# A layer norm's first two weight pieces, token tile by token tile, with splits, squares and roots in other places

## The reference

```
u = rmsnorm(x, norm_mix);  proj = u @ w_in          # then attention, convolution, gates
x = x + merged @ w_mix_out
u = rmsnorm(x, norm_mlp)
x = x + square(relu(u @ w_mlp_up)) @ w_mlp_down
```

## Time and profile before

| | us |
|---|---|
| median of 3 runs | 1827.13 (1826.56 to 1827.42) |
| the profiled execution, its own time | 1827.84 |
| its span | 1826.4 |
| PE busy in the span | 1733.0 (95%) |
| mean granted TensorE clock, as a share of 2.4 GHz | 0.978 |

### The profile page before, as it was taken

One profiled execution on the slowest core, in us unless ns is written; L12 is line 12 of the kernel. 1 busy time (PEld: TensorE's weight loads), 2 busy tenths in 40 slices (PEclk: granted clock), 3 DMA queues, 4 the chain that ended last, 5 costly groups with the idle time before them and its releaser, 6 DMA issues.

```text
span 1826.4 us, 33244 instructions
## 1 busy us (share of the span) xinstructions
PE 1733.0 (95%) x11638; PEld 1592.1 (87%) x11638; DVE 1352.7 (74%) x2358; ACT 911.6 (50%) x1601; POOL 63.8 (3%) x116
## 2 busy tenths in 40 slices
PE   6999899998999899988988999999999999999996
PEld 5999799988899788977867999999999978888885
DVE  5985778876876678868665699997888856666665
ACT  3344344443354434443544455567777644455543
POOL 0000011000000112100000000000000000000000
PEclk9999999998999999998988999999999999999999
DMA  5655587753544599852325355554344455555553
GB/s 200 206 191 181 177 301 270 264 189 117 168 150 161 179 337 299 268 185 82 116 81 184 128 177 179 184 185 150 130 137 138 136 167 193 195 192 189 194 194 138
DMA packets 92041, 333.87 MB, mean 183 GB/s; under 512 B 11048, under 2 KB 11224, under 8 KB 91504
## 3 DMA queue, kind: packets, MB, share of 16 engines
q1 hardware_dynamic: 80064, 289.06, 47.1%
q0 software_dynamic: 10912, 39.38, 6.5%
q10 hardware_dynamic: 976, 4.19, 0.6%
HBM read 330.46 MB, written 6.07 MB: 184 GB/s over the span
## 4 chain that ended last, share of the span: by engine, by line
PE 78%; DVE 14%; ACT 3%; issue 3%; DMA 2%; DVEq 0%; SPq 0%; ACTq 0%
PE bank L199 23%; PE bank L200 23%; PE bank L201 23%; DVE Z L84 6%; DVE w_lo L180 4%; PE bank L1617 3%; DMA raw<-stream 1%; PE bank L249 1%; ACT w_hi L178 1%; ACT space L84 1%; PE bank L1226 1%; DVE st L84 1%; DVE x L84 1%; DVE u_lo L84 1%; PE bank L453 1%
## 5 line engine op out<-in xcount | busy, mean ns | idle before, releaser
L180 DVE TENSOR_TENSOR w_lo<-raw,w_hi 128x1024 fp32r<-128x1024 f32 x546 | 661.4, 1221 | 183.2 <-ACT w_hi L178 181.6
L178 ACT ACTIVATE w_hi<-raw 128x1024 fp32r<-128x1024 f32 x546 | 573.9, 1052 | 289.0 <-PE bank L201 212.1
L199 PE MATMUL bank<-u_hi,w_hi 128*128 128x256 f32 x2416 | 703.6, 291 | 9.4 <-DVE w_lo L180 3.5
L201 PE MATMUL bank<-u_hi,w_lo 128*128 128x256 f32 x2416 | 688.7, 285 | 0.0
L200 PE MATMUL bank<-u_lo,w_hi 128*128 128x256 f32 x2416 | 688.7, 285 | 0.0
L199 PEld LDWEIGHTS bank<-u_hi,w_hi 128*128 128x128 f32 x2416 | 469.2, 194 | 23.8 <-issue 10.6
L200 PEld LDWEIGHTS bank<-u_lo,w_hi 128*128 128x128 f32 x2416 | 468.6, 194 | 4.7 <-issue 2.4
L201 PEld LDWEIGHTS bank<-u_hi,w_lo 128*128 128x128 f32 x2416 | 468.2, 194 | 0.0
L199 PE MATMUL bank<-w_hi,a_hi 128*128 128x512 f32 x768 | 300.7, 391 | 3.7 <-DVE a_lo L936 1.8
L200 PE MATMUL bank<-w_lo,a_hi 128*128 128x512 f32 x768 | 300.2, 391 | 0.0
L201 PE MATMUL bank<-w_hi,a_lo 128*128 128x512 f32 x768 | 299.5, 390 | 0.0
(11 more groups left out here) (263 smaller groups left out, 1659.4 us busy)
## 6 DMA issues: line engine op xcount, KB each, us to landing
raw<-stream SPq DMA_DIRECT2D x546, 512.0 KB, 3.3
gate<-w_ada POOLq DMA_DIRECT2D x48, 512.0 KB, 6.5
space<-b_ada POOLq DMA_DIRECT2D x6, 512.0 KB, 4.6
t_rows<-t_by_distance POOLq DMA_DIRECT2D x8, 256.0 KB, 3.9
rpb_rows<-rpb_pad POOLq DMA_DIRECT2D x8, 224.0 KB, 3.9
gains<-gains POOLq DMA_DIRECT2D x3, 512.0 KB, 4.8
bias_a<-t_rows POOLq DMA_DIRECT2D x1, 1536.0 KB, 11.1
bias_b<-rpb_rows POOLq DMA_DIRECT2D x16, 96.0 KB, 7.9
```

The source lines that it names most:

```text
L178: nc.scalar.activation(w_hi[:, s, :], raw[:, s, :], ACT.Copy).then_inc(s_hi, 1)
L180: nc.vector.tensor_tensor(w_lo[:, s, :], raw[:, s, :], w_hi[:, s, :].bitcast(F32), ALU.subtract).then_inc(s_split, 1)
L199: M.matmul(o, lh, rh, start=start, stop=False, skip_group_check=True)
L201: return M.matmul(o, ll, rh, start=False, stop=stop, skip_group_check=True)
```

## The change

- `first_pieces` and `token_tile_b` take the place of `piece_b` for the two pieces behind each of the four layer norms: piece 1 over tile 0, piece 2 over tile 0, piece 1 over tile 1, piece 2 over tile 1. Each matmul has 128 moving columns, so there are 96 in place of 48.
- `second_tile`, a generator that is advanced behind each of the two tile 0 parts, issues the rest: first the split of a held piece's successor, the transposes and squares of tile 1 or 0; then the second transposes, the other splits and squares. `split` of the held pieces' slots is thereby issued later.
- `squares` comes ahead of the two pieces' end; `token_roots` stays behind them.
- The transposes of tile 0 come one held piece earlier where three are held.
- At the start x is loaded in two DMAs of 512 KB by token tile, not in four of 256 KB.
- The two `held_pieces` calls of the second block issue their splits after the held pieces instead of among them; only PE instructions lie between the two places.

```
+        def token_tile_b(o, s, tt, ready):
+
+            cols = slice(tt * P, (tt + 1) * P)
+            for k in range(KD):
+                PE.wait(*ready[tt][k // 4])
+                i = mm3(o[:, cols], w_hi[:, s, k * P:(k + 1) * P], w_lo[:, s, k * P:(k + 1) * P],
+                        u_hi[:, k, cols], u_lo[:, k, cols], k == 0, k == KD - 1)
+            return i
+
+        def first_pieces(outs, ready, beside):
+
+            c, marks = at["piece"], []
+            for j, o in enumerate(outs):
+                nc.tensor.wait_ge(s_split, dyn(RING) + (c + j + 1))
+                token_tile_b(o, (c + j) % RING, 0, ready)
+                next(beside)
+            for j, o in enumerate(outs):
+                i = token_tile_b(o, (c + j) % RING, 1, ready)
+                at["piece"] += 1
+                marks.append(used(i))
+                if j:
+                    split(c + j + AHEAD)
+            return marks
...
                         i.then_inc(s_used, 1)
-                        if j < count - 1:
-                            split(c + AHEAD + 1 + j)
-                        if j == count - 2:
-                            late()
+                        if j == count - 1:
+                            bank_marks[NT - 1][1] = (s_used, dyn(RING) + (c + count))
+                        next(steps, None)
                 if tt == 0:
-                    halfway()
-            bank_marks[NT - 1][1] = (s_used, dyn(RING) + (c + count))
+                    next(steps, None)
+            return c + AHEAD + 1, count - 1
...
-            held_pieces(count, lhs, acc, lambda: (tile(0, 0), tile(0, 1)),
-                        lambda: turn_chunk(0, 0, gained[0, 0], ready))
-            turn_chunk(0, 1, gained[0, 1], ready)
+            def steps():
+                tile(0, 0), tile(0, 1)
+                yield
+                turn_chunk(0, 0, gained[0, 0], ready)
+                lower_next()
+                yield
+                if count > 2:
+                    turn_chunk(0, 1, gained[0, 1], ready)
+                    yield
+
+            beside = steps()
+            c, waiting = held_pieces(count, lhs, acc, beside)
+            if count == 2:
+                turn_chunk(0, 1, gained[0, 1], ready)
             lower_next()
             tile(1, 0)
+            tile(1, 1)
+            return ready, second_tile(ready, gained, marks, list(range(c, c + waiting + 1)))
+
+        def second_tile(ready, gained, marks, splits):
+
+            if splits:
+                split(splits.pop(0))
             turn_chunk(1, 0, gained[1, 0], ready)
+            squares(x, space_junk, 5, marks, 0)
             lower_next()
-            tile(1, 1)
-            lower_next()
+            yield
             turn_chunk(1, 1, gained[1, 1], ready)
             lower_next()
-            return ready, marks
+            while splits:
+                split(splits.pop(0))
+            got_sums[0] = squares(x, space_junk, 5, marks, 1)
+            yield
...
-        load_x(0, 0)
+        nc.sync.dma_start(x[:, 0, :], x_in[0:P, :]).then_inc(s_x[0], 16)
         nc.sync.dma_start(gains[:, 0, :], gains1[0:1, :].partition_broadcast(P).rearrange(
             "p a n -> p (a n)")).then_inc(s_gain0, 16)
         nc.sync.dma_start(kept[:, :], kept_in).then_inc(s_kept, 16)
-        load_x(1, 0)
         load_first(0)
-        load_x(0, 1)
-        load_x(1, 1)
+        nc.sync.dma_start(x[:, 1, :], x_in[P:2 * P, :]).then_inc(s_x[1], 16)
         for s in range(1, RING):
...
-        u_ready = [() for _ in range(KD)]
+        x_marks = [[(s_x[tt], 16)] * 2 for tt in range(NT)]
+        u_ready, gained = [[(), ()], [(), ()]], {}
+        space_junk = work[:, :, :].rearrange("p a n -> p (a n)")
         for n in range(2):
-            for tt in range(NT):
-                m = gain_chunk(x, gains[:, 0, :], tt, n, (s_gain0, 16), x_marks[tt][n])
-                turn_chunk(tt, n, m, u_ready)
-                if n or tt:
-                    lower_next()
-            if n == 0:
-                split(0)
+            m = gain_chunk(x, gains[:, 0, :], 0, n, (s_gain0, 16), x_marks[0][n])
+            turn_chunk(0, n, m, u_ready)
+            if n:
+                lower_next()
         lower_next()
-        for c in range(1, AHEAD):
-            split(c)
+        split(0)
+        for n in range(2):
+            gained[1, n] = gain_chunk(x, gains[:, 0, :], 1, n, x_marks[1][n])
+        first_u = u_ready, second_tile(u_ready, gained, x_marks, list(range(1, AHEAD + 1)))
...
-                take(4)
-                m = piece_b([bank[4][:, 0:T]], *U, ready=u_ready)
+                take(4), take(5)
+                m, iq_m = first_pieces([bank[4][:, 0:T], bank[5][:, 0:T]], *first_u)
...
-                for tt in range(NT):
-                    m = squares(x, work[:, :, :].rearrange("p a n -> p (a n)"), 5, x_marks, tt)
-                yield
-                m = token_roots(m)
+                m = token_roots(got_sums[0])
...
-            up(0, tile0 + 0, True)
-            up(1, tile0 + 1, True)
-            for tt in range(NT):
-                m = squares(x, work[:, :, :].rearrange("p a n -> p (a n)"), 5, x_marks, tt)
+            for q, m in enumerate(first_pieces([bank[4][:, 0:T], bank[5][:, 0:T]], *first_u)):
+                up(q, tile0 + q, m)
+            m = got_sums[0]
```

More of the change, by code:

```diff
@@ L235, in run @@
                 pass
-        ss_marks, norm_late, junk_mark = [], [], [None]
+        ss_marks, norm_late, junk_mark, got_sums = [], [], [None], [None]
         free = {}
@@ L315, in turn_chunk @@
                        bank[b][:, :].rearrange("p (k n) -> p k n", k=4), ACT.Copy)
-            norm_late.append((b, n, rows, m1, i, ready))
+            norm_late.append((b, n, tt, m1, i, ready))
         def lower_next():
-            b, n, rows, m1, i, ready = norm_late.pop(0)
+            b, n, tt, m1, i, ready = norm_late.pop(0)
+            rows = slice(tt * P, (tt + 1) * P)
             m = VE.go((m1, i), V.tensor_tensor, u_lo[:, 4 * n:4 * n + 4, rows],
@@ L323, in lower_next, with held_pieces @@
             free[b] = (m1, m)
-            for k in range(4 * n, 4 * n + 4):
-                ready[k] += (m1, m)
-        def held_pieces(count, lhs, acc, halfway, late):
+            ready[tt][n] = (m1, m)
+        def held_pieces(count, lhs, acc, steps):
             c, slots = at["piece"], []
@@ L347, in held_pieces @@
                         i.then_inc(s_used, 1)
-                        if j < count - 1:
-                            split(c + AHEAD + 1 + j)
-                        if j == count - 2:
-                            late()
+                        if j == count - 1:
+                            bank_marks[NT - 1][1] = (s_used, dyn(RING) + (c + count))
+                        next(steps, None)
                 if tt == 0:
-                    halfway()
-            bank_marks[NT - 1][1] = (s_used, dyn(RING) + (c + count))
+                    next(steps, None)
+            return c + AHEAD + 1, count - 1
         def added_and_gained(count, lhs, acc, x, gain, scale=None):
-            ready, marks, gained = [() for _ in range(KD)], [[None, None], [None, None]], {}
+            ready, marks, gained = [[(), ()], [(), ()]], [[None, None], [None, None]], {}
             def tile(tt, n):
@@ L606, in build @@
         store_ada(ADA_PER_LAYER - 1)
-        x_marks = [[(s_x[2 * tt + n], 16) for n in range(2)] for tt in range(NT)]
-        u_ready = [() for _ in range(KD)]
+        x_marks = [[(s_x[tt], 16)] * 2 for tt in range(NT)]
+        u_ready, gained = [[(), ()], [(), ()]], {}
+        space_junk = work[:, :, :].rearrange("p a n -> p (a n)")
         for n in range(2):
-            for tt in range(NT):
-                m = gain_chunk(x, gains[:, 0, :], tt, n, (s_gain0, 16), x_marks[tt][n])
-                turn_chunk(tt, n, m, u_ready)
-                if n or tt:
-                    lower_next()
-            if n == 0:
-                split(0)
+            m = gain_chunk(x, gains[:, 0, :], 0, n, (s_gain0, 16), x_marks[0][n])
+            turn_chunk(0, n, m, u_ready)
+            if n:
+                lower_next()
         lower_next()
-        for c in range(1, AHEAD):
-            split(c)
+        split(0)
+        for n in range(2):
+            gained[1, n] = gain_chunk(x, gains[:, 0, :], 1, n, x_marks[1][n])
+        first_u = u_ready, second_tile(u_ready, gained, x_marks, list(range(1, AHEAD + 1)))
         m = VE.go((), V.memset, one[:, :], 1.0)
@@ L638, in main_part @@
                     b = 5 - n % 2
-                    take(b)
-                    for e in range(parts):
+                    if n:
+                        take(b)
+                    for e in range(0 if n else 1, parts):
                         m = piece_b([bank[b][:, e * T:(e + 1) * T]], *U)
@@ L909, in build @@
             VE.wait((s_gain, 48))
-            u_ready, x_marks = added_and_gained(
+            first_u = added_and_gained(
```

(26 more changed lines are left out.)

3 lines of the change are left out of this document (removed).

## The result

The changed kernel takes 1850.01 us (median of 4 runs, 1848.54 to 1851.05) against 1826.85 for the kernel before beside it: a ratio of 1.0127, interval 1.0109 to 1.0144. It is slower, by 23.2 us. The forecast was 1840 (1818 to 1866) with slower as the likeliest sign. The time is that of the case in which **both** middles fall to the low clock (1851), to which I had given 8 in a hundred. (To fall is to go from the granted clock of 1.00 to that of 0.50.)

What follows compares the result with a forecast made beforehand. PE, busy for 95% of the span, was taken as the bound. With one middle falling, start +8.6, middles +9.4 and -1.0, turn -4.0 gave +13.0 on 1827.13: 1840 us, range 1818 to 1866.

Steps and rivals of the forecast that it cites:

- Price: At each place, 96 matmuls of 128 columns take 0.107 us each at 2.4 GHz, 0.206 at 1.2 GHz, set by weight loads.
- Rivals 1, 2 and 3: 1: half-price matmuls, 1807 (14%); 2: load-bound, clock rises during the pieces, 1820 (12%); 3: four times the cycles, 1862 (22%).
- the step: In the matmul price: halving the columns gains nothing at 1.2 GHz, so the 128 x 128 load sets the pace.
- Start: First layer norm: PE starts 2.6 us earlier, roots' wait goes, but the clock stays low: 8.6 us later in all.
- Middles: Both middles: pieces start 4.8 us earlier; gain 1.7 and 1.0 without a fall, loss 9.4 and 10.1 with one.
- I give each middle four in ten: Chance of the clock falling in each middle, its 2.15 us idle lying between 1.84 (no fall) and 2.22 (fall).
- the "235.2" there: Middle 1: the time given for the end of its third piece without a fall, counted as a gain of 1.0 us.
- Turn: At the turn: pieces start earlier, R without the roots' wait, the fourth piece ends at 432.4, 4.0 us earlier.
- The step that PE waits for tile 0's second `u_lo`: At the turn: `u_lo` ends at 413.75, PE starts at 413.8 in place of 417.36, having idled 1.4 us.
- Moved splits: Held pieces' later splits cost nothing on the middles' path; SP's later loads taken as 0, at most 2 us each.
- second block: Second block: ACT and DVE keep the same order as before, so 0.
- Squares: At the turn: the squares lie on ACT between its `u_hi`s, hidden beside PE's 10 us.

Runs made afterwards that it cites:

- the best version: Changed kernel with whole pieces at start and middles, tiles at the turn only, filler in the middles and zeros at the start: 1811.46 us, ratio 0.9919.
- filler: Changed kernel plus eight 512-column products on a ready weight piece in each middle's wait for x: 1832.94 us, ratio 1.0029.
- zeros: Changed kernel with filler in the middles, plus twelve and twelve products of zeros at the start: 1822.04 us, ratio 0.9969.
- the 11.2 of the order: Changed kernel's new order, but whole pieces (48 matmuls of 256 columns) at all four places: 1815.86 us, ratio 0.9938 to the kernel before.
- the 2.1 at the turn: Whole-pieces version in the new order, with the tile order kept at the turn only: 1813.81 us, ratio 0.993 to the kernel before.
- the splits' own experiment: Whole-pieces version in the new order, with the splits of the held pieces put back among the held pieces: 1815.78 us, ratio 0.994.

## Why the prediction was right, and where not

**The account.** From the change's 1850.0 to the best version's 1811.5: 17.1 is the low clock in the middles (filler), 10.9 the low clock at the start (1832.9 to 1822.0, zeros), and 10.6 what the tile order costs at full clock at start and middles (1822.0 to 1811.5; in the traces 2.8 at the start, 31.81 against 29.00, and 3.9 at middle 1, of which 0.3 is a longer wait for `qT`). That is 38.5 in all. The change is 23.2 slower than the kernel before and not 38.5, for against these stand the 11.2 of the order, the 2.1 at the turn, and 2.4 that filler and zeros still give with whole pieces (1813.8 to 1811.5): 22.8 is left.

- *Price.* Taken 0.107 and 0.206 from transposes; measured 0.113 and 0.214. Rivals 1, 2 and 3 are out. That it is the load which sets this pace is argued, not shown: at the low clock 128 and 256 columns go at one pace (0.214 here, 0.217 in the earlier trace rows), as the step would have it, and the earlier trace rows has it for float32; but a matmul that takes two cycles for a column below 256 columns would give the same 0.214, and no run has fp32r matmuls of 64 columns to tell the two apart. The Trainium skill (page "TensorE: Matmul & The Clock Gate", section "Back-to-back issue gap") has 81 ns for such a pair; the trace does not agree for these operands. The Trainium skill (same page, section "Weight-path perf modes") has a fast weight load where the type is not FP32; it is not seen here, as 0.113 us at 2.4 GHz is 271 cycles for 128 columns.
- *Start.* +8.6 forecast, +8.5 measured, by the steps as written: the piece at 12.91 (said 13.7), no rise of the clock in 96 narrow matmuls, the third piece in 4.70 (said 4.7), R without a wait. The closeness is part luck, as the earlier start (-0.8) and the dearer matmuls (22.1 for 21.4) cancel.
- *Middles.* The piece came at 228.72, which is 220.2 with the start's 8.5; the wait was 1.98 (said 2.15). A fall cost +9.7 and +8.9 (said +9.4, +10.1; the "235.2" there is 635.2, and the 1.0 from it stands). **The step that failed is "I give each middle four in ten"**: both fell, so 1840 was 10 too low, though the price of a fall was nearly right. The reasoning behind it compared idle times, with 1.84 as one that does no harm and 2.22 as one that does. The runs show that this does not order the cases: after 1.98 the clock fell in the change, and did not with 256 columns behind the same 1.98; after 1.98 and 1.99 in two executions of one code it fell once at each middle and once stayed. The four executions of the change lie within 2.5 us, so likely both middles fell in all of them.
- *Turn.* -4.0 forecast, -5.2 measured. The step that PE waits for tile 0's second `u_lo` was wrong: k below 4 needs chunk (0,0) alone, ready long before, and PE starts without idling at 430.38, 5.2 earlier than before (said 3.5). That also took away the idle time that I had counted (1.4). The rest was right: R without a wait, clock at 1.00.
- *Moved splits* and *second block* at 0: right in all (-0.1 in the splits' own experiment, 20.8 at 720 us and at the end), but each is a sum of parts that cancel. *Squares*, "hidden beside PE's 10 us": right, and worth 5.4 us by the R waits they remove.

The sum with both falls by the record is 1851, against 1850.0.

## What to carry to other kernels

Where 128 x 128 fp32r weights are loaded for each matmul, 128 moving columns cost nearly as much as 256 (0.113 against 0.120), so splitting a stream by token tile nearly doubles its price; of the four places it paid at the turn alone, by 2.1 us, not clear of noise. In every low stretch up to 700 us the clock rose only in the wider matmuls behind the narrow ones. So count with 0.214 and not 0.113 behind a wait like these of 2 us, or keep PE busy through the wait (a few products on data already there cost nothing and gave 17 and 11 us). And separate the parts before judging a change: here the order of side work was worth 11 us and was hidden under 34 of loss.

## What the runs showed that I had not expected

- The fall is not a function of the code. Eight executions of the kernel with zeros at the start took 1831 to 1854 us, in two groups (1831 to 1836, 1847 to 1854), and two profiles show opposite middles low. Nor is it so for narrow streams alone: behind one and the same wait of 2.68 us for `w_lo` with 256-column matmuls behind it (843.29 before, 864.01 after) the clock fell in the changed kernel's execution and not in the other. With the idle time filled, nine executions of the same matmuls lie within 4.6 us. The Trainium skill (page "TensorE: Matmul & The Clock Gate", section "What's actually happening") says that the count of slow matmuls varies between runs of one kernel; the runs agree, and the spread is much larger here, as a narrow stream that fell stayed low to its end (20 us and more). What the executions near 1850 lose beyond two middles was not profiled and stays open.
- PE is at 100% in a low stretch (18.40 of 18.40 us at 0.50). A full PE did not bring the clock up there. With the moving columns doubled and nothing else changed, no stretch from 18 to 700 us was low; as falls differ between executions, it is the nearness of all ten (mean clock 0.984 to 0.988) that speaks against chance.
- In the changed kernel PEclk reads 1.00 for the first 40 us, although the pace of 0.214 is that of 1.2 GHz; I had expected to read 0.50. The window of the start's pieces in the changed kernel:

```profile
12.91:34.90 21.99, 21.99 (x104) 21.99 (x105) 9.46 (x25) 8.12 (x15) 0.00 (x0) 1.00 0.42 149
```

At the start of a program the pace is to be read, not the column.
